# Four outer products a call in a retention layer, a reordered start, and the last prompt state moved into the joint

## What is computed

```python
# prompt: chunkwise, state starts at zero
o = (q k^T * decay) v ;  S_prompt = sum_j (k_j * k_dec_j) v_j^T
# samples: 8 sequences of 4 tokens, each with a state S of 256 x 512
o = (q k^T * decay) v + (q * q_dec) S
S_new = gamma**4 * S + sum_j (k_j * k_dec_j) v_j^T
```

## Time and profile before

| | |
|---|---|
| time, median of 3 runs | 994.88 us (994.68 to 995.05) |
| the profiled execution | 994.74 us |
| its span, first to last instruction | 992.8 us |
| PE busy | 971.7 us, 98% of the span |
| DVE busy | 595.6 us, 60% |
| ACT busy | 432.0 us, 44% |
| POOL busy | 35.5 us, 4% |
| data moved | 206.63 MB, mean 208 GB/s |

### The profile page before, as it was taken

The page is one execution under the profiler, slowest core; times in us unless marked ns, Lnnn a source line. Parts: engine busy times, 40 slices in busy tenths (PEclk is TensorE's granted clock), DMA queues, the critical chain, the costliest instruction groups (busy, mean ns, idle before and its releaser), DMA issues. The chain is left out here.

```text
span 992.8 us, 17813 instructions
## 1 busy us (share of the span) xinstructions
PE 971.7 (98%) x7580; PEld 894.5 (90%) x7580; DVE 595.6 (60%) x769; ACT 432.0 (44%) x544; POOL 35.5 (4%) x68
## 2 busy tenths in 40 slices
PE   8999999999999999999999999999999999999996
PEld 8988998657999999999988878788799999999996
DVE  6756654666686553334875767675683775553343
ACT  5231224676655443333542534435344554443331
POOL 0310000000000000000001010100100000000000
PEclk9999999999999999999999999999999999999998
DMA  9887759856344444443556858685764254444421
GB/s 353 332 288 264 271 198 349 313 187 250 127 170 171 169 169 166 159 164 146 205 182 243 323 186 303 222 291 196 272 248 170 86 209 164 162 161 160 166 79 48
DMA packets 50702, 206.63 MB, mean 208 GB/s; under 512 B 3536, under 2 KB 3920, under 8 KB 35024
## 3 DMA queue, kind: packets, MB, share of 16 engines
q1 hardware_dynamic: 45216, 182.58, 51.6%
q0 software_dynamic: 5424, 23.15, 6.2%
HBM read 181.39 MB, written 24.33 MB: 207 GB/s over the span
## 5 line engine op out<-in xcount | busy, mean ns | idle before, releaser
L610 PE MATMUL banks<-hH,wH 128*128 128x288 f32 x1248 | 375.7, 301 | 4.3 <-DVE hL L1616 2.8
L1229 ACT ACTIVATE wH<-raw 128x2048 fp32r<-128x2048 f32 x116 | 222.3, 1916 | 360.9 <-PE banks L612 358.3
L1607 DVE TENSOR_TENSOR wL<-raw,wH 128x2048 fp32r<-128x2048 f32 x113 | 258.8, 2290 | 188.3 <-ACT wH L1229 188.0
L612 PE MATMUL banks<-hH,wL 128*128 128x288 f32 x1248 | 368.6, 295 | 0.0
L611 PE MATMUL banks<-hL,wH 128*128 128x288 f32 x1248 | 368.5, 295 | 0.0
L610 PEld LDWEIGHTS banks<-hH,wH 128*128 128x128 f32 x1248 | 236.4, 189 | 19.8 <-issue 10.2
L611 PEld LDWEIGHTS banks<-hL,wH 128*128 128x128 f32 x1248 | 235.6, 189 | 0.4
L612 PEld LDWEIGHTS banks<-hH,wL 128*128 128x128 f32 x1248 | 235.1, 188 | 0.0
L612 PE MATMUL banks<-aH,wL 128*128 128x288 f32 x512 | 151.8, 296 | 0.0
L610 PE MATMUL banks<-aH,wH 128*128 128x288 f32 x512 | 151.3, 296 | 0.0
L611 PE MATMUL banks<-aL,wH 128*128 128x288 f32 x512 | 149.3, 292 | 0.0
(11 more groups left out here) (292 smaller groups left out, 996.4 us busy)
## 6 DMA issues: line engine op xcount, KB each, us to landing
raw<-wst SPq DMA_DIRECT2D x120, 1024.0 KB, 4.9
cache_sb<-kcache SPq DMA_DIRECT2D x14, 1024.0 KB, 7.6
sslot<-state SPq DMA_DIRECT2D x11, 1024.0 KB, 7.8
sstate_out<-sslot POOLq DMA_DIRECT2D x11, 1024.0 KB, 6.8
raw<-vcache SPq DMA_DIRECT2D x6, 1024.0 KB, 10.1
w_area<-vcache SPq DMA_DIRECT2D x6, 1024.0 KB, 13.0
raw<-state SPq DMA_DIRECT2D x5, 1024.0 KB, 8.4
sstate_out<-raw POOLq DMA_DIRECT2D x5, 1024.0 KB, 5.5
```

The costliest lines, as they stand in the source:

```text
L610: nc.tensor.matmul(out[:, m, :], wH[:, u % 2, c], hi[:, k, :], start=first, stop=False)
L612: return nc.tensor.matmul(out[:, m, :], wL[:, u % 2, c], hi[:, k, :], start=False, stop=last)
L1229: nc.scalar.activation(wH[:, at % SPL, :], raw[:, raw_slot(at), :], ACT.Copy).then_inc(h_round, 1)
L1607: nc.vector.tensor_tensor(wL[:, at % SPL, :], raw[:, raw_slot(at), :], wH[:, at % SPL, :].bitcast(F32), ALU.subtract).then_inc(l_split, 1)
```

## The change

**Outer products.** `outers(u, p)` now makes all four products of a unit in one call: two into banks 6 and 7, two into the pair of G banks that strip p doesn't use (`outer_banks`). There is one call per unit, always at j = 0, of strips p = HEAD_AT[h] + 1 to + 4 (`UNIT_AT`). It waits for the result of strip p - 1 to be taken out. `update` runs at j = 0 for the half in the G banks and at j = 1 for banks 6 and 7; strip p + 1 waits for the former. `read_states` stands at i = 3, 6, 9, 10. Two entries of `U_AT` are later.

**Start.** x comes in three groups (2, 2, 4 tiles), strip 1 in halves, strip 2 ahead of `mat`. The first product of each half does high x high, then low weight x high, then high x low. The second is done by halves too, with its low weights last. The sum of squares moves into the third product. Strips 2 and 3 are rounded and split ahead of the root, and later splits stand one strip further ahead. 16 instead of 14 multiplications stand before it.

**Last prompt state.** `prompt_state(3, z)` leaves the strips and goes into the joint b = 3, into banks 6 and 4, around `spread_root`, with 7 multiplications behind it in place of 5 + 14. ACT's copies go into `pre_norm`, POOL's stores behind the last unit.

```diff
+UNIT_AT = {HEAD_AT[h] + 1 + k: 4 * h + k for h in range(NHR) for k in range(4)}
-U_AT = (4, 4, 7, 11, 11, 12, 13, 16, 16, 17, 18, 21, 21, 22, 23, 25)
+U_AT = (4, 4, 7, 11, 11, 12, 14, 16, 16, 17, 19, 21, 21, 22, 23, 25)
-N_RUN_FIRST = 14
+N_RUN_FIRST = 16
+N_RUN_STATE = 7
+        def outer_banks(p):
+            at = 2 * ((p + 1) % 2)
+            return banks[:, 6:8, :], banks[:, at:at + 2, :]
...
+                for half in range(2):
+                    ks = range(4 * half, 4 * half + 4)
+                    pe.wait_ge(h_round if half else half_round, 1)
+                    for k in ks:
+                        pe.wait_ge(hx_round, k + 1)
+                        for m in range(2):
+                            part_product(0, out, wH, hH, m, k, start=k == 0)
+                    pe.wait_ge(l_split if half else half_split, 1)
...
+                if b == 3:
+                    prompt_state(NHR - 1, 0)
+                    spread_root(b - 1)
+                    prompt_state(NHR - 1, 1)
+                    warm(N_RUN_STATE, 5)
...
-            def outers(u, e):
+            def outers(u, p):
                 h, g, z = u // 4, u // 2 % 2, u % 2
                 pe.wait_ge(r_stack, 2 * h + 2)
-                if u or e:
-                    pe.wait_ge(r_updated, 2 * u + e)
-                for i in range(2):
-                    r = slice(64 * e + 32 * i, 64 * e + 32 * i + 32)
-                    mm = nc.tensor.matmul(banks[:, 6 + i, :], kst[r, g, z * P:z * P + P], vst[r, g, :], start=True, stop=True)
+                if u:
+                    pe.wait_ge(r_updated, 2 * u)
+                pe.wait_ge(g_dve, GBUF + GD_RET + p)
+                for i in range(4):
+                    r = slice(32 * i, 32 * i + 32)
+                    mm = nc.tensor.matmul(outer_banks(p)[i // 2][:, i % 2, :], kst[r, g, z * P:z * P + P], vst[r, g, :],
+                                          start=True, stop=True)
...
             for p in range(4, N_RETIN):
                 pe.wait_ge(g_dve, GBUF + GD_RET + (p - 3 if p < 6 else p - 1))
+                if p - 1 in UNIT_AT:
+                    pe.wait_ge(r_updated, 2 * UNIT_AT[p - 1] + 1)
...
-                if 3 <= i <= 8:
-                    update(4 * h + (i - 3) // 2, (i - 3) % 2)
-                if i == 10:
-                    update(4 * h + 3, 0)
+                if p in UNIT_AT and j < 2:
+                    update(p, 1 - j)
```

More of the change, by code:

```diff
@@ L577, in _, with store_prompt_state @@
             nc.gpsimd.memset(kpad[:, :, :, :], 0.0).then_inc(r_zero, 1)
-            for h in range(NHR):
+            def store_prompt_state(h):
                 for z in range(2):
@@ L581, in _ @@
                     pool.dma_start(pstate_out[h, z * P:(z + 1) * P, :], ps_sb[:, z, :]).then_inc(ps_stored, 16)
+            for h in range(NHR):
+                if h < NHR - 1:
+                    store_prompt_state(h)
                 for u in range(4 * h, 4 * h + 4):
@@ new lines, in first_product, with part_product, second_product @@
+                mm.then_inc(strip_used, 1)
+            def part_product(u, out, w, h, m, k, start=False, stop=False):
+                c = slice(k * SC + m * P, k * SC + m * P + P)
+                return nc.tensor.matmul(out[:, m, :], w[:, u % 2, c], h[:, k, :], start=start, stop=stop)
+            def second_product(out):
+                for half in range(2):
+                    ks = range(4 * half, 4 * half + 4)
+                    pe.wait_ge(h_round if half else w1_round, 1 + half)
+                    for m in range(2):
+                        for k in ks:
+                            part_product(1, out, wH, hH, m, k, start=k == 0)
+                            part_product(1, out, wH, hL, m, k)
+                    pe.wait_ge(l_split if half else w1_split, 1 + half)
+                    for m in range(2):
+                        for k in ks:
+                            mm = part_product(1, out, wL, hH, m, k, stop=k == KT - 1)
@@ L1065, in head_scores @@
                 mm.then_inc(r_scored, 1)
[L1067 to L1072, removed]
             def out_prompt(h, half):
@@ L1235, in round_x, with copy_state @@
                 nc.scalar.activation(hH[:, k, :], x[:, k, :], ACT.Copy, scale=gain(layer, norm, k)).then_inc(hx_round, 1)
+            def copy_state(h, z):
+                if h and z == 0:
+                    act.wait_ge(ps_stored, 16 * 2 * h)
+                    act.wait_ge(os_turned, h if h < NHR - 1 else NHR)
+                act.wait_ge(r_state, 2 * h + z + 1)
+                nc.scalar.activation(ps_sb[:, z, :], banks[:, 5 if h < NHR - 1 else STATE_BANK[z], :],
+                                     ACT.Copy).then_inc(r_scopied, 1)
             def pre_norm(b, layer, norm, s):
+                if b == 3:
+                    copy_state(NHR - 1, 0)
                 for k, n in X_GROUPS:
@@ L1750, in _ @@
                     split_x(0, k, 0, 0)
-            split_strip(1, 1)
+            for ready, count, c, done in ((w1_round, 1, slice(0, HALF_STRIP), w1_split),
+                                          (h_round, 2, slice(HALF_STRIP, KT * SC), l_split)):
+                dve.wait_ge(ready, count)
+                nc.vector.tensor_tensor(wL[:, 1, c], raw[:, 1, c], wH[:, 1, c].bitcast(F32), ALU.subtract).then_inc(done, 1)
+            split_strip(SPL, SPL)
             dve.wait_ge(xsq0, 2)
@@ L2091, in head_step @@
                     sum_tiles(h, 0)
-                    update(4 * h + 3, 1)
                 if i == 12:
```

162 lines of the change are left out of this document (89 added, 73 removed).

## The result

| | before | after |
|---|---|---|
| time, median | 994.96 us (994.68 to 996.39, 4 runs) | 984.19 us (983.86 to 984.47, 4 runs) |
| the profiled execution | 994.74 us | 984.47 us |
| its span | 992.8 us | 982.5 us |

The account below looks back on a forecast made before the run. PE was taken as the bound, busy for 971.7 of 992.8 us. Terms of 6.4, 2.5 and 1.8 summed to 10.7 off the profiled 994.74, so 984.0, with the median at 984.2; range 980.8 to 988.5.

Parts of the forecast that it names:

- outer products, net: Strips with head work: 16 of 32 calls dropped, gross 8.4 us, less 2.0 lost to DVE's order, net 6.4.
- last prompt state, net: Two calls, 3.45 us, leave the strips, and the root in the joint turns 0.95 late: net 2.5, bounds 1.8 and 3.4.
- start: First strips: PE starts at 8.1 without idle time and strip 1 by halves is no wait; 1.8 us taken.
- the first crossing: Head 0 to 1: DVE's low parts come later for `turn_pad_k`, so PE goes on 0.4 us later than before.
- rival 1: Outer products: four tiles don't run at once, a call costs 0.86 us; total 990.1 us, chance 8%.
- The crossings: From one head to the next, DVE's bunched updates make PE late by 0.4, 0.6 and 1.0 us, 2.0 in all.
- Rival 2: DVE bounds every head, with waits inside heads too, 0.9 us more in each of four; 987.8 us, chance 20%.
- The early case: Start: the clock rises by 8.5 us and ACT and DVE feed PE, first strip ends at 14.6; gain 2.7.
- low case: Start: full clock comes at 12.0 us as before, the first strip ends at 16.25; gain 1.0.
- high case: Start: full clock by 8.5 us, with PE fed so that the first strip ends at 14.6; gain 2.7.
- Rival 3: Crossings take up the shift and the clock rises early: 2.0 and 0.9 us more gained, 981.3 us, chance 20%.
- Counted 0: New waits in the strips, for an update at a strip's head, slots or SP's later stores, were put at no cost.

Follow-up runs that it names:

- the call of eight: The changed kernel with each call's four outer products issued twice, the same values written again: 987.35 us, ratio 0.9918.
- the update in the gap: The changed kernel with the second update of a head's last unit moved between the centring and the sum behind ACT's squares: 982.01 us, ratio 0.9869.

## Why the prediction was right, and where it was right by luck

The forecast was 984.2, the measurement 984.19. The three parts, taken one after the other, make 6.6 + 2.35 + 1.7 = 10.65, forecast 10.7. But two of the three terms were off by half a microsecond to one, in opposite directions, and that they cancel is luck.

| | forecast | measured |
|---|---|---|
| outer products, net | 6.4 | 6.6 |
| last prompt state, net | 2.5 | 1.7 |
| start | 1.8 | 2.35 |

**Outer products: the steps held, apart from the first crossing.** With the outer products alone, PE gains 2.0, 2.0, 2.2 and 2.1 us in the four heads, forecast 2.1 each. The call of four was put at 0.45 and is 0.43 to 0.44; rival 1, with its 0.86, falls by the call of eight, where four more cost 0.23. The crossings were priced at 0.4, 0.6 and 1.0. At the second and third PE loses 0.7 and 1.1. The place of the second was wrong: I had worked it out from the low parts ahead of `turn_pad_k`, and the wait stands earlier, at `turn_v`, behind DVE's result (609.15, 0.55). At the first I had misread. There PE's wait of 0.24 ahead of 564.10 was not one for DVE's low parts, which were ready at 563.3; it ended behind ACT's copy, which both kernels need:

```profile
562.95 1.00 ACT L1492 ACTIVATE vtok_r<-banks 128x1024 f32<-128x1024 f32 x1
```

In the changed kernel ACT's copy is over at 559.35, DVE's low parts at 559.85, and L1109 starts at 559.90, 0.19 behind the product before it, where L1042 took 0.37. So the low parts had 0.65 us in hand that I hadn't counted, and PE loses nothing there against before; with the update in the gap it wins 0.3. The wait was one for several semaphores, and I had looked at one of them.

**Rival 2 fell.** It wanted waits on DVE inside the heads, 0.9 more in each. The gain inside the heads came in full, and beside the crossings the list of waits has only what stood there before: 1.0 ahead of head 0, and L1192 with 0.75 where L1129 had 0.6. The Trainium skill ("TensorEngine Tiling (Array Packing)", section "PSUM Bottleneck") says that packing tiles doesn't speed up the emptying of the banks. The trace agrees in this much: an update still takes 1.22 us, DVE's idle time ahead of 22 updates fell from 28.7 to 7.9, and each of the crossings' losses stood behind such an update; the bound itself wasn't reached, as DVE is busy for 60% of the span.

**Last prompt state: 0.8 too much.** The joint was right: the root came 1.0 later, forecast 0.95, and PE's stretch there lost 1.0. The step that failed is the one that took both calls at their full 3.45 us "off PE" in the strips. I looked for what a late step holds up, and not for what an early one meets: the first call had hidden ACT's table load, gate and copy of `vst` from PE, and 0.72 came back as a wait of L1179: 3.45 - 0.72 - 1.0 = 1.7. With a bound for this in the sum the term would have been 1.8.

**Start: 0.55 too little by the medians, 0.35 by the traces, and near by a mean of two cases.** From strip 4 to retention PE is 2.15 to 2.2 ahead of the kernel before. I had chosen between full rate from 12.0 (1.0) and from 8.5 (2.7), and taken 1.8, which neither case gives. The early case came: the trace's record of the granted clock begins, at full, at 7.63. There the sizing failed the other way: the second strip's product was to start at 14.6 and starts at 15.11. Six groups of eight products at 1.06 would have ended at 14.4; the first takes 1.56, at the pace of ACT's roundings, and the fourth 1.26. I had written that ACT and DVE feed PE so that it ends at 14.6; ACT doesn't. The mean of a low case that didn't come and a high case put too high is luck. That the early clock alone, in the old order, is worth nothing was in the rows too, since 17.19 came from DVE's split: the profiled executions take 994.74 with products slow until 12.12 and 995.20 with full rate from 9.48. The lower end of my range, the new order at the slow rate, no run shows. The Trainium skill ("TensorE: Matmul & The Clock Gate", Part 1) says that the number of slow products differs between runs. The trace agrees: the same first instructions gave products 0.24 apart until 12.12 in the kernel before and none with the outer products alone.

**Rival 3 came by half.** The clock rose early, which brought 0.35 to 0.55 more than forecast and not 0.9. The crossings took up only the first shift: 0, 0.7 and 1.1 are lost there, 1.8 of the 2.0 forecast.

**Counted 0, and so it was:** PE waited for no update at a strip's head, for no slot, and SP's later stores held up no strip.

## What to carry to other kernels

When work is taken off the bounding engine, ask of the instruction that now comes earlier which of its inputs the removed work had covered; look at all producers, not at the one that waited before. When updates are bunched, put them where their engine waits anyway: the gap of 1.2 us took one update per head and gave back 2.2 us. And where a part is late because another stands ahead of it in the queue, move by halves: two products ahead of the root make it 0.14 later than before, four 1.0.

## What the runs showed of the hardware

Four products of 32 rows and 512 columns into four banks cost PE no more than two: 0.43 us start to start, and four more on top 0.23, so that nearly half of a call is a fixed part of it.

The clock at the start can rise and fall again before the first product. The spacing of products tells the level (0.24 us is 1.2 GHz, 0.13 is 2.4). The granted clock agrees where the trace has a record of it, but ahead of the first record the views print 1.00 whatever the rate. That is what the earlier trace rows met: in the kernel before the record begins at 12.14 us, where the spacing halves. It begins at 8.45 in the old order with 18 multiplications, at 6.84 with the outer products alone, at 7.63 in the changed kernel and at 5.51 in that with 14, at full clock each time. With the start taken back it begins at 5.48; PE's last multiplication there ends at 6.61, and the views have the fall (stretch, length, busy us per engine, clock, share, GB/s):

```profile
5.60:8.80 3.20, 1.02 (x13) 0.82 (x10) 1.45 (x2) 1.84 (x3) 0.00 (x0) 1.00 1.02 402
9.00:12.20 3.20, 2.96 (x12) 2.99 (x13) 2.79 (x6) 3.20 (x7) 0.00 (x0) 0.50 1.01 421
```

The clock fell at 8.89, while PE stood (6.61 to 9.24), and rose again at 12.30, with products running. In the kernel with 14 multiplications and the new order it rose at 5.51 too, PE stood for 1.26 until 7.92, and the clock stayed. With the outer products alone it rose at 6.84, PE stood for 1.59, and it stayed as well. When it first rises differs between kernels with the same instructions up to there, and what sets that moment stays open.
